# Rounding the memory attention's operands beside its query units, and the queries' scale in a pad

## The reference, cut to what matters

```python
def memory_cross_attention(hn, memn, w_q, w_k, w_v, w_o):
    q = (hn @ w_q).reshape(bsz, seq, 4, 256)
    k = (memn @ w_k).reshape(bsz, 256, 4, 256)
    v = (memn @ w_v).reshape(bsz, 256, 4, 256)
    s = jnp.einsum('blhd,bmhd->bhlm', q, k) * 256 ** -0.5
    p = jax.nn.softmax(s, axis=-1)
    o = jnp.einsum('bhlm,bmhd->blhd', p, v).reshape(bsz, seq, 1024)
    return o @ w_o
```

## Time and profile before

| | us |
|---|---|
| median of 3 runs | 2342.94 |
| the runs | 2340.88, 2342.94, 2348.97 |
| the profiled execution, its own time | 2345.94 |
| its span, first to last instruction | 2344.1 |
| around the span | 1.84 |
| TensorE busy | 2201.4 (94%) |
| mean granted TensorE clock | 0.976 of full speed |

### The profile page before, as it was taken

One profiled execution on the slowest core, in us unless ns is written; L12 is line 12 of the kernel. 1 busy time (PEld: TensorE's weight loads), 2 busy tenths in 40 slices (PEclk: granted clock), 3 DMA queues, 4 the chain that ended last, 5 costly groups with the idle time before them and its releaser, 6 DMA issues.

```text
span 2344.1 us, 41787 instructions
## 1 busy us (share of the span) xinstructions
PE 2201.4 (94%) x17205; PEld 2059.1 (88%) x17205; DVE 1589.0 (68%) x2104; ACT 1008.1 (43%) x1198; POOL 205.9 (9%) x202
## 2 busy tenths in 40 slices
PE   8898998999999989999999979999999987999998
PEld 6675996899999878999999867999999986889998
DVE  8987654556578677655579778655556986866554
ACT  4113445443444554433444455443345445544432
POOL 3762002100000110000000210000000011000000
PEclk9999999999999999999999989999999998999999
DMA  7688674565555433565565322455545532335551
GB/s 248 235 286 302 243 268 145 176 200 179 190 167 179 127 103 114 168 192 179 171 183 167 118 72 91 148 174 180 198 146 173 158 126 72 107 110 162 186 191 71
DMA packets 290483, 393.09 MB, mean 168 GB/s; under 512 B 8518, under 2 KB 256668, under 8 KB 283676
## 3 DMA queue, kind: packets, MB, share of 16 engines
q1 hardware_dynamic: 285620, 383.53, 50.1%
q10 hardware_dynamic: 3624, 6.31, 0.8%
q0 software_dynamic: 1088, 1.10, 0.2%
HBM read 387.66 MB, written 3.15 MB: 167 GB/s over the span
## 4 chain that ended last, share of the span: by engine, by line
PE 80%; DVE 11%; ACT 4%; issue 2%; DMA 2%; ACTq 0%; POOL 0%; DVEq 0%
PE L L852 64%; PE M L852 3%; PE L L1103 2%; DVE w_rest L434 2%; PE M L986 2%; PE L L1089 2%; ACT w_high L428 1%; PE M L1339 1%; DVE work L2635 1%; DVE m L2002 1%; PE L L1116 1%; DMA raw<-in_w_ada 1%; PE L L1172 1%; DVE n_rest L2011 1%; DVE soft L2116 1%
## 5 line engine op out<-in xcount | busy, mean ns | idle before, releaser
L852 PE MATMUL L<-n_high,w_high 128*128 128x256 f32 x3360 | 956.0, 285 | 17.6 <-DVE w_rest L434 5.8
L852 PE MATMUL L<-n_rest,w_high 128*128 128x256 f32 x3360 | 940.5, 280 | 0.0
L852 PE MATMUL L<-n_high,w_rest 128*128 128x256 f32 x3360 | 940.3, 280 | 0.0
L434 DVE TENSOR_TENSOR w_rest<-raw,w_high 128x2048 fp32r<-128x2048 f32 x293 | 671.2, 2293 | 239.0 <-PE L L852 231.4
L428 ACT ACTIVATE w_high<-raw 128x2048 fp32r<-128x2048 f32 x293 | 561.0, 1915 | 369.4 <-PE L L852 334.0
L852 PEld LDWEIGHTS L<-n_high,w_high 128*128 128x128 f32 x3360 | 638.5, 190 | 38.0 <-issue 29.5
L852 PEld LDWEIGHTS L<-n_high,w_rest 128*128 128x128 f32 x3360 | 639.1, 190 | 0.0
L852 PEld LDWEIGHTS L<-n_rest,w_high 128*128 128x128 f32 x3360 | 637.6, 190 | 0.8
L852 PE MATMUL L<-hid_high,w_high 128*128 128x256 f32 x768 | 218.5, 284 | 3.1 <-DVEq L2436 3.1
L852 PE MATMUL L<-hid_high,w_rest 128*128 128x256 f32 x768 | 217.5, 283 | 0.0
L852 PE MATMUL L<-hid_rest,w_high 128*128 128x256 f32 x704 | 199.4, 283 | 0.0
(11 more groups left out here) (408 smaller groups left out, 2777.4 us busy)
## 6 DMA issues: line engine op xcount, KB each, us to landing
raw<-in_w_in SPq DMA_DIRECT2D x116, 1024.0 KB, 5.5
raw<-in_w_ffn SPq DMA_DIRECT2D x99, 1024.0 KB, 5.2
raw<-in_w_ada SPq DMA_DIRECT2D x32, 1024.0 KB, 6.4
raw<-in_w_out SPq DMA_DIRECT2D x16, 1024.0 KB, 5.2
raw<-in_w_gate SPq DMA_DIRECT2D x11, 1024.0 KB, 5.4
raw<-in_w_up SPq DMA_DIRECT2D x11, 1024.0 KB, 5.3
raw<-in_w_down SPq DMA_DIRECT2D x11, 1024.0 KB, 4.9
work<-in_w_ada SPq DMA_DIRECT2D x8, 1024.0 KB, 7.6
```

Of the source, the lines that this page charges most:

```text
L434: nc.vector.tensor_tensor(w_rest[:, u.first % 2, :], raw[:, u.first % 4, :], w_high[:, u.first % 4, :].bitcast(F32), ALU.subtract).then_in ...
L852: ins = mm(dst, a, b, start=first and i == 0, stop=last and i == 2, skip_group_check=skip)
```

## The change

- `kv` gets a second name of rounded type, `kv_r`, for the same memory.
- `q_scale` is no tensor of its own but the first 16 words of the pad `behind_n`. All tensors named after it start 64 bytes lower: `rstd`, `m`, `gate`, `hid_high`, `hid_rest`, `b_high`, `b_rest`, `work`, `b_land`, and what shares their memory.
- In the memory attention four K and four V copies are held. The high part of K lies in `hc_r`, that of V in `work_r` at 4096; their rests are written over K and V in `kv_r`. So all of K and V is split at task -1, in the order of heads (K, Q, V of head 0, of head 1, then K and V of heads 2 and 3); Q of heads 2 and 3 follows at tasks 0 and 2.
- ScalarE does these copies head by head behind the evacuations of mem_q's units, and the first exponential behind the third unit's.
- TensorE makes the scores of tasks 0 and 1 ahead of mem_q's fourth unit; its wait for mem_q's evacuation stands now before the first fill.
- VectorE takes the first two negative maxima within mem_q's third unit.

```diff
--- before.py
+++ after.py
@@ -207,7 +207,10 @@
...
         spill = nc.dram_tensor("spill", (P, DC * T), F32).ap()
-        kv = sb("kv", [P, 5632])
+        over = ExitStack()
+        with over:
+            kv = over.enter_context(nc.sbuf_tensor("kv", [P, 5632], F32))
+        kv_r = sb("kv_r", [P, 5632], F32R)
         ident = sb("ident", [P, P])
@@ -231,7 +234,7 @@
...
         soft = sb("soft", [P, 4, 4])
-        q_scale = sb("q_scale", [P, 2, 8])
+        q_scale = behind_n[:, 0:16].rearrange("p (a h) -> p a h", a=2)
         rstd = sb("rstd", [P, T])
@@ -293,11 +296,11 @@
...
 
-        STORE = {"mem": dict(k=("w", 4096), v=("w", 5120), q=("w", 6144), turned=7168, turned_rest=7680, exp=8192, step=256),
+        STORE = {"mem": dict(k=("c", 0), v=("w", 4096), q=("w", 6144), turned=7168, turned_rest=7680, exp=8192, step=256),
                  "gqa": dict(k=("h", 0), v=("h", 1024), q=("h", 1536), turned_rest=1024, exp=5504, turned=7040, step=512),
...
         SHARE = {"mem": dict(k=1, q=1, v=1), "gqa": dict(k=4, q=2, v=4), "diff": dict(k=1, q=1, v=1)}
-        BUFFERS = {"mem": dict(k=1, q=2, v=1), "gqa": dict(k=1, q=2, v=1), "diff": dict(k=2, q=1, v=1)}
+        BUFFERS = {"mem": dict(k=MEM_HEADS, q=2, v=MEM_HEADS), "gqa": dict(k=1, q=2, v=1), "diff": dict(k=2, q=1, v=1)}
         WORDS = {"mem": dict(k=512, q=512, v=512), "gqa": dict(k=512, q=256, v=256), "diff": dict(k=512, q=256, v=512)}
@@ -563,7 +566,12 @@
...
             other = hx_r if key[0] == "c" else hc_r
-            buf = {"w": work_r, "q": qd_r, "h": other[:, :, :].rearrange("p a t -> p (a t)")}[home]
+            buf = {"w": work_r, "q": qd_r, "h": other[:, :, :].rearrange("p a t -> p (a t)"),
+                   "c": hc_r[:, :, :].rearrange("p a t -> p (a t)")}[home]
+            if key == "mem" and what != "q":
+                rest = {"k": kv_r[:, 0:2048].rearrange("p (c t) -> p c t", c=DC)[:, 2 * h:2 * h + 2, :],
+                        "v": kv_r[:, 2048:4096].rearrange("p (a n) -> p a n", a=2)[:, :, 2 * h * P:2 * (h + 1) * P]}[what]
+                return shaped(buf[:, at + h * w:at + (h + 1) * w], like), rest
             slot = n % BUFFERS[kind][what]
@@ -582,16 +590,18 @@
...
                     events = []
-                    for what in "kqv":
+                    operands = [(what, h) for what in "kqv" for h in range(0, len(firsts), SHARE[kind][what])]
+                    if kind == "mem":
+                        operands.sort(key=lambda x: x[1])
+                    for what, h in operands:
                         share, held = SHARE[kind][what], BUFFERS[kind][what]
-                        for h in range(0, len(firsts), share):
-                            free = h - (held - 1) * share
-                            when = firsts[free] + (1 if what == "v" else -2) if free > 0 else -1
-                            if when == at:
-                                done += 1
-                                events.append((what, h, tasks[firsts[max(free, 0)]], done))
-                                for i in range(share):
-                                    NEED[key, what, h + i] = done
+                        free = h - (held - 1) * share
+                        when = firsts[free] + (1 if what == "v" else -2) if free > 0 else -1
+                        if when == at:
+                            done += 1
+                            events.append((what, h, tasks[firsts[max(free, 0)]], done))
+                            for i in range(share):
+                                NEED[key, what, h + i] = done
                     SPLITS[key, at] = events
@@ -987,7 +997,7 @@
...
 
-            def attention(key, before, parts_of, values_of, beside={}, clear={}, between=None):
+            def attention(key, before, parts_of, values_of, beside={}, clear={}, between=None, ahead=None):
 
@@ -1042,7 +1052,9 @@
...
                 maps = kind_of(key) == "diff"
-                if maps:
+                if ahead is not None:
+                    ahead(lambda: (score(tasks[0]), score(tasks[1])))
+                elif maps:
                     score_maps(tasks[0], tasks[1])
@@ -1274,18 +1286,18 @@
...
             mid("norm", 2)
-            cols_linear("mem_q", chunk=normed_chunk(2))
-            evacuated(pe, "mem_q")
 
...
                 pe.wait_ge(fill_in[i % 2], 16 * (i // 2 + 1))
+                if i == 0:
+                    evacuated(pe, "mem_q")
                 late_modulation(i, fill_slot[i % 2], L[:, 2, :], fill_done)
...
                       lambda h, bank: [(bank[:, d * T:(d + 1) * T], slice(d * P, (d + 1) * P)) for d in range(2)],
-                      between=fill)
+                      between=fill, ahead=lambda scores_: cols_linear("mem_q", before={3: scores_}, chunk=normed_chunk(2)))
 
@@ -1563,14 +1575,16 @@
...
 
-            def attention(key, beside={}):
+            def attention(key, beside={}, ahead=None):
 
...
 
-                def split(at):
+                def split(at, only=None):
                     for what, h, x, _ in SPLITS[key, at]:
+                        if only is not None and h != only:
+                            continue
                         if what != "v" and x["g"]:
@@ -1595,8 +1609,11 @@
...
                       turned_bank[x["group"] % 2][:, 0:nk].rearrange("p (c q) -> p c q", q=P), ACT.Copy).then_inc(probs_T_high, 1)
-                split(-1)
-                exponentials(0, tasks[0])
+                if ahead is None:
+                    split(-1)
+                    exponentials(0, tasks[0])
+                else:
+                    ahead(lambda h: split(-1, h), lambda: exponentials(0, tasks[0]))
                 if kind_of(key) == "diff":
@@ -1766,9 +1783,15 @@
...
             ada_out(4, M[:, 2, :])
-            out_to("mem_q", zu, scale=float(D // MEM_HEADS) ** -0.5)
-            evacuated(act, "mem_q")
-            attention("mem")
+
+            def mem_q_out(split, first):
+
+                def rounded(j):
+                    act.wait_ge(bank_free[j], after("mem_q", j))
+                    split(j)
+                out_to("mem_q", zu, scale=float(D // MEM_HEADS) ** -0.5,
+                       beside={0: lambda: rounded(0), 1: lambda: rounded(1), 2: lambda: (rounded(2), first()), 3: lambda: rounded(3)})
+            attention("mem", ahead=mem_q_out)
             multiplied(act, "mem_q")
@@ -2105,7 +2128,7 @@
...
 
-            def attention(key, out_of, negl=None, beside={}):
+            def attention(key, out_of, negl=None, beside={}, ahead=None):
 
@@ -2145,8 +2168,11 @@
...
                     out_of(x["h"], head_bank).then_inc(o_ready, 1)
-                negative_max(tasks[0])
-                negative_max(tasks[1])
+                if ahead is None:
+                    negative_max(tasks[0])
+                    negative_max(tasks[1])
+                else:
+                    ahead(lambda: (negative_max(tasks[0]), negative_max(tasks[1])))
                 for i, x in enumerate(tasks):
@@ -2409,8 +2435,8 @@
...
             norm(2, hx, lambda c: col("xattn_norm_g", c), zero)
-            linear("mem_q")
-            attention("mem", lambda h, bank: V.tensor_copy(o_mem[:, 2 * h:2 * h + 2, :].rearrange("p a t -> p (a t)"), bank))
+            attention("mem", lambda h, bank: V.tensor_copy(o_mem[:, 2 * h:2 * h + 2, :].rearrange("p a t -> p (a t)"), bank),
+                      ahead=lambda first: linear("mem_q", beside={2: first}))
             n_split(o_mem, NHIGH_EVENTS["o_mem"])
```

## The result

The changed kernel takes 2322.56 us (median of 4 runs, 2316.63 to 2325.74) against 2345.95 us (4 runs): a ratio of 0.9899, interval 0.9869 to 0.9929. It is faster, by 23.4 us, more than twice what was forecast and outside the stated range.

A forecast was written before the change was run, and what follows sets the result against it. TensorE carries 80% of the chain of waits, so time is won only where it stands still or runs slowly. The staging gives 10.6 us, the pad nothing: 2342.94 to 2332.3, predicted 2332.5 us, range 2325 to 2341.

The forecast's parts named there:

- (5): The pad: buffers behind the queries' scale start 64 bytes lower; taken as no effect, with ends of 21 us either way.
- mirror case: Matmuls on the shifted buffers speed up to 0.1136 us each, 21 us faster, 2311 us; chance 0.03.
- the rival: Shifted buffers get slower: a larger address unit counts, 3264 matmuls lose a step, 10.4 us slower, 2353 us; chance 0.05.
- (1) to (4): Memory attention: early scores, K and V rounded in mem_q, first exponential inside mem_q, loop paced by loads; 10.6 us less.
- (4): Walk of the attention loop: POOL waits gone, ada loads rule, one slot turns in 6.0 us, mem_o starts at 415.8.
- the bound: POOL subtractions held by DVE at 1.95 us each: fills 2 and 3 come 1.2 us later, gain 9.4 us.
- the walk: Attention loop's rebuilt timeline: fills 1, 3, 5, 7 wait for loads; fills 2, 4, 6 are never behind.
- the stall of 4.09 us: TensorE's wait for POOL ahead of the first scores: goes with the early scores, and the drop of the clock with it.
- the first rival: The clock drops anyway in the attention, from TensorE's 1 us holes: costs 4 us, gain 6.6 us, 2336.3 us; chance 0.17.
- the forecast's 8 us: Scatter between runs, 2340.88 to 2348.97 us, used in setting the range.

The follow-up runs named there:

- e1: Kernel before with only the queries' scale moved into the pad, so later buffers start 64 bytes lower, attention staged as before; ratio to before 0.9935.
- e5: Changed kernel with the weights' rounded tensors 64 bytes higher, n_high and hid_high not moved; ratio to before 1.0085.
- e7: Changed kernel with GpSimd's subtractions from K of head 1 on waiting for VectorE's rest of mem_q's last unit; ratio to before 0.9894, stage 46.85 us.
- e2: Changed kernel with the queries' scale back in its own place, so the staging alone; ratio to before 0.9949, stage 47.84 us.
- e9: Changed kernel without the loads of fills 2 to 7, all matmuls kept, some results wrong; ratio to before 0.9875, stage 44.15 us.
- e10: e7 with a third slot, in m, for the fills' loads; ratio to before 0.9883, stage 42.95 us.
- e8: Changed kernel with operands still rounded in mem_q, but first two scores, their maxima and first exponential behind mem_q; ratio to before 0.9954, stage 57.65 us.
- e4: Kernel before with 128 bytes added ahead of rstd, so later buffers keep their remainder by 128; ratio to before 0.9976.
- e6: Changed kernel with n_high and n_rest at remainder 32 by 128, hid, b and work at 96, weights at 0; ratio to before 1.0060.
- e3: Kernel before with 64 bytes added ahead of rstd, so later buffers move up to remainder 64 by 128; ratio to before 0.9927.

## Why the prediction was wrong

- **(5), the pad: this step failed.** It read "after a shift of exactly 64 bytes hid_high is still 4 bytes past. I take nothing.", and so put the term at 0. The start addresses were summed from widths, without the rounding to 32 bytes and the first tensor's place, and the reason looked for was in the operand alone. The runs put 15 us there (e1: 15.2, interval 10 to 20), and e5 shows that the place of the weights belongs to it. The stated mirror case had the sign and, at 21 us, too much; it got a chance of 0.03, although the rows showed 0.0064 us between two tensors and 3264 matmuls on shifted ones. The unit that the rival named, "some larger unit, of which the shift changes the remainder", was the right kind: 128 bytes, and a change from 0 to 64. Its sign was the mirror's.
- **The staging (1) to (4): mechanism right, size off.** 8.7 us in the stage against 10.6. Fill 0 came 20.0 us behind the second unit, forecast 18.75; fill 7 at 42.2, forecast 40.3. Of these 1.9 us, 1.1 are the fourth unit's wait for w_rest. Another 0.7 come at fill 4, whose load took 5.59 us to land where the forecast had 4.9 to 5.04 (5.46 in e7, 5.39 in e2).
- **The port.** The Trainium skill's rule (SBUF — State Buffer, "SBUF: two separate sides"), that a two-input VectorE operation and a GpSimd operation exclude each other, was weighed the wrong way round. The trace agrees with the exclusion: VectorE's subtraction ended 2.15 us behind the last of GpSimd's, about the 2.29 us that it takes undisturbed. But the bound priced GpSimd held by VectorE; in the run GpSimd had six subtractions in a row and VectorE was held, 5.1 us on one subtraction. TensorE's third unit and the scores covered most of it, so 1.1 us reached the path.
- **(4), the loads rule.** Right: four waits of 0.45, 1.15, 1.06 and 0.81 us for loads and none on GpSimd; e9 and e10 show what they cost, 3.6 and, beside e7, 3.9 us. Three of the four lie in the slot of fills 2, 4 and 6, which the walk called "never behind".
- **The clock.** 1.00 through the stage, so the first rival is wrong. That the stall of 4.09 us and the clock behind it are one term was right. e8 agrees from the other side: with stalls of 2.3 to 2.6 us the clock fell again and the stage won nothing, though the held subtraction and one long load have a share in that.
- **Scatter.** ffn_up goes at 114.5 or 119.0 us per 1008 matmuls, in the same kernel from layer to layer and above. One such stretch is 4.5 us. This wasn't in the range; the forecast's 8 us came from three runs, over all sets it was 25 us.

The range of 2325 to 2341 had no room for the pad: the staging alone (e2) took 2333.65 us and lies in it.

Not settled: why a stretch falls on 0.1136 or 0.1180 us a matmul at one and the same address; and whether the distance or each operand's own place counts. Of the pad's 15 us, 8.2 are read off the down units of e1 (four times 528 matmuls) and about 4 off those on b; the rest is within the interval.

## What to carry to other kernels

Where a three-product matmul stream is dense, read the starts of weights and moving operands from the built program and try them 64 bytes apart by 128, with the weights at a multiple of 128; the sign is a tensor whose matmuls are slower than another's in every layer, for a single stretch also varies by itself (114.5 or 119.0 us here). Rounding the operands ahead of a stage may be worth little by itself (e8): the first dependent step (here scores, maximum, table load, exponential) has to leave the path with it, since its stall can take the clock down. Before putting GpSimd subtractions side by side, look for a VectorE operation with two inputs that will be issued among them.

## What was not expected of the hardware

- Time per 128 x 256 matmul in dense stretches by the distance of the moving operand from the weights: a multiple of 256 bytes, 0.1200 to 0.1208 us (before, e2, hid_high); an odd multiple of 128, 0.1186 to 0.1200 (e4, e5); 32 or 96 by 128, 0.1183 to 0.1192 (e6); 64 by 128, 0.1136 to 0.1186 (changed, e1, e3), so that single stretches of different distances overlap and only sums over a kernel tell them apart.
- The granted clock fell beside stalls of TensorE of 2.30, 2.39 and 2.62 us (e8), and stayed at 1.00 with stalls up to 1.47 us (changed kernel).
- One VectorE subtraction of 2.29 us took 7.37 us beside GpSimd subtractions that followed one another, and 3.84 us when these paused.
